# Differential attention: order of the key's sum of squares, a weight conversion and a weight split within a head

## The reference

```
q, k, v = split(h @ w_in, 3)                      # 8 heads, q and k in two halves of 64
q = rms_norm(q, q_g);  k = rms_norm(k, k_g)       # over each half's 64 features
q1, q2, k1, k2 = partial_rope(...)                # rotary on 16 of the 64
a = softmax(mask(q1 k1^T / 8)) - lam * softmax(mask(q2 k2^T / 8))
o = rms_norm(a @ v, sub_g) * (1 - lam_init)       # per head
out = o @ w_out
```

## Time and profile before

| | us |
|---|---|
| median of 3 runs | 2301.11 (2300.15 to 2301.57) |
| profiled execution, device time | 2300.4 |
| its span, first to last instruction | 2298.6 |
| PE matmul busy | 2221.3 (97%) |
| PE weight load busy | 1756.8 (76%) |
| DVE busy | 1391.9 (61%) |
| ACT busy | 795.7 (35%) |

### The profile page before, as it was taken

The page is one execution under the profiler, slowest core; times in us unless marked ns, Lnnn a source line. Parts: engine busy times, 40 slices in busy tenths (PEclk is TensorE's granted clock), DMA queues, the critical chain, the costliest instruction groups (busy, mean ns, idle before and its releaser), DMA issues.

```text
span 2298.6 us, 28503 instructions
## 1 busy us (share of the span) xinstructions
PE 2221.3 (97%) x10128; PEld 1756.8 (76%) x10128; DVE 1391.9 (61%) x2100; ACT 795.7 (35%) x1161; POOL 0.2 (0%) x4
## 2 busy tenths in 40 slices
PE   7999999999999999999999999989899999999998
PEld 5777688888886666788888867777678888888886
DVE  5666654554447776655454475577754557888744
ACT  4445432222225554322222223446622323222222
POOL 0000000000000000000000000000000000000000
PEclk9999999999999999999999999999999999999999
DMA  4111133333331111233333322222223332333332
GB/s 128 55 55 55 46 92 101 91 100 90 99 96 56 55 55 46 78 96 99 96 96 95 100 66 65 53 59 65 55 81 103 92 98 87 99 100 93 94 101 87
DMA packets 368642, 188.29 MB, mean 82 GB/s; under 512 B 8968, under 2 KB 368313, under 8 KB 368569
## 3 DMA queue, kind: packets, MB, share of 16 engines
q1 hardware_dynamic: 368569, 187.30, 28.5%
HBM read 185.18 MB, written 2.10 MB: 81 GB/s over the span
## 4 chain that ended last, share of the span: by engine, by line
PE 83%; DVE 10%; ACT 4%; issue 3%; DMA 0%; DVEq 0%; SPq 0%; ACTq 0%
PE lin L1548 73%; PE S L1572 1%; DVE dmax L992 1%; PE ob L1603 1%; ACT w_hi L520 1%; PE S L1585 1%; DVE conv L1256 1%; PE ob L1697 1%; DVE w_lo L877 1%; PE S L1811 1%; PE S L1590 1%; PE S L1575 1%; DVE prob L1005 0%; PE ob L1837 0%; DVE q_raw L1014 0%
## 5 line engine op out<-in xcount | busy, mean ns | idle before, releaser
L520 ACT ACTIVATE w_hi<-raw 128x1024 fp32r<-128x1024 f32 x361 | 381.0, 1056 | 825.4 <-PE lin L1548 817.3
L877 DVE TENSOR_TENSOR w_lo<-raw,w_hi 128x1024 fp32r<-128x1024 f32 x361 | 441.0, 1222 | 207.4 <-ACT w_hi L520 206.5
L1548 PE MATMUL lin<-h_hi,w_hi 128*128 128x512 f32 x1928 | 498.1, 400 | 7.4 <-DVE exact L1435 2.8
L1548 PE MATMUL lin<-h_lo,w_hi 128*128 128x512 f32 x1928 | 480.5, 391 | 0.0
L1548 PE MATMUL lin<-h_hi,w_lo 128*128 128x512 f32 x1928 | 478.3, 390 | 0.0
L1548 PEld LDWEIGHTS lin<-h_hi,w_hi 128*128 128x128 f32 x1928 | 362.3, 190 | 95.4 <-issue 14.1
L1548 PEld LDWEIGHTS lin<-h_hi,w_lo 128*128 128x128 f32 x1928 | 360.9, 188 | 74.8 <-issue 0.5
L1548 PEld LDWEIGHTS lin<-h_lo,w_hi 128*128 128x128 f32 x1928 | 360.2, 188 | 74.8 <-issue 0.8
L1548 PE MATMUL lin<-gu_lo,w_hi 128*128 128x512 f32 x528 | 131.4, 389 | 0.0
L1548 PE MATMUL lin<-gu_hi,w_lo 128*128 128x512 f32 x528 | 131.4, 389 | 0.0
L1548 PE MATMUL lin<-gu_hi,w_hi 128*128 128x512 f32 x528 | 131.4, 389 | 0.0
(11 more groups left out here) (311 smaller groups left out, 2241.8 us busy)
## 6 DMA issues: line engine op xcount, KB each, us to landing
raw<-in_w_in_dram SPq DMA_DIRECT2D x108, 512.0 KB, 3.8
raw<-in_w_gate_dram SPq DMA_DIRECT2D x44, 512.0 KB, 3.7
raw<-in_w_up_dram SPq DMA_DIRECT2D x44, 512.0 KB, 3.8
raw<-in_ffn_up_dram SPq DMA_DIRECT2D x44, 512.0 KB, 3.8
raw<-in_w_down_dram SPq DMA_DIRECT2D x32, 512.0 KB, 3.8
raw<-in_w_out_dram SPq DMA_DIRECT2D x24, 512.0 KB, 3.8
raw<-in_ffn_down_dram SPq DMA_DIRECT2D x16, 512.0 KB, 3.9
raw<-in_w_down_dram SPq DMA_DIRECT2D x16, 384.0 KB, 3.3
```

Of the source, the lines that this page charges most:

```text
L520: act.activation(w_hi[u.slot][:, :, :], raw[u.slot][:, :, :], ACT.Copy).then_inc(hi_ready, 1)
L877: dve.tensor_tensor(w_lo[u.slot][:, :, :], raw[u.slot][:, :, :], w_hi[u.slot][:, :, :].bitcast(f32), ALU.subtract).then_inc(lo_ready, 1)
L1548: ins = pe.matmul(acc, (wh, wh, wl)[part][:, k, :], (hi, lo, hi)[part][:, k0 + k, :], start=first and part == 0 and k == 0, stop=last and ...
```

## The change

Three pieces of queue order move, one on each of ACT, DVE and PE; no instruction is added or removed. On ACT `hi(u + 3)` goes behind `keep_turned(n, 3)`. On DVE `split(u + 2)` goes behind `mix(n, 2)`. On PE `qk_sum(n + 1, 1)` goes behind `turn_diff(n, 3)` and the value's product part 1, directly ahead of `weigh`. Head 7 keeps its order.

```diff
@@ ACT, head
                     keep_turned(n, 2)
                     if not last:
                         qk_square(n + 1, 1)
+                    keep_turned(n, 3)
+                    if not last:
                         hi(u + 3)
-                    keep_turned(n, 3)
-                    if not last:
                         qk_scale(n + 1, 1)
@@ DVE, head
                     maxima(n, 3)
+                    mix(n, 2)
                     if not last:
                         split(u + 2)
-                    mix(n, 2)
                     mix(n, 3)
@@ PE, head
                     turn_diff(n, 2)
                     if not last:
                         linear(n + 1, 2, (0,))
+                    turn_diff(n, 3)
+                    if not last:
+                        linear(n + 1, 2, (1,))
                         qk_sum(n + 1, 1)
-                    turn_diff(n, 3)
-                    if not last:
-                        linear(n + 1, 2, (1,))
                     weigh(n, last)
```

More of the change, by code:

```diff
@@ L645, in head @@
                         qk_square(n + 1, 1)
-                        hi(u + 3)
                     keep_turned(n, 3)
                     if not last:
+                        hi(u + 3)
                         qk_scale(n + 1, 1)
@@ L1737, in head @@
                         linear(n + 1, 2, (0,))
-                        qk_sum(n + 1, 1)
                     turn_diff(n, 3)
@@ L1741, in head @@
                         linear(n + 1, 2, (1,))
+                        qk_sum(n + 1, 1)
                     weigh(n, last)
```

## The result

| | before | after |
|---|---|---|
| median of 4 runs, us | 2301.22 (2300.15 to 2301.57) | 2284.94 (2283.82 to 2286.33) |
| profiled execution, us | 2300.4 | 2286.33 |
| its span, us | 2298.6 | 2284.5 |
| mean granted clock of PE in it | 0.988 | 0.988 |
| first scores of head 1 to first scores of head 7, us | 172.83 | 161.56 |

The ratio is 0.9935, with an interval of 0.992 to 0.9949. The heads' part of it, the last row, came out at 11.27 us, where the steps gave 9.35 + 1.80 = 11.15.

What follows compares the result with a forecast made beforehand. PE sets the pace and loses time by waiting. Heads 1 to 5 save 5 x 1.87 = 9.35 us, head 6 1.80, head 0 1.35, head 7 0: together 12.5, from 2301.1 to 2288.6 us; range 2286.0 to 2293.0.

Steps and rivals of the forecast that it cites:

- `diff` 2 from the last small maximum: DVE, head 3: `diff` 2 ends 1.59 us after the last small maximum's start, as in head 7, 1.14 us earlier.
- split of DVE costs `diff` 3: DVE: with the split behind `mix` 2, `diff` 3 still ends at 801.20; cost taken as 0, upper bound 0.2 us.
- `turn_diff` 3 waits for `diff` 3: PE, head 3: `turn_diff` 3 could start at 801.13 but `diff` 3 allows 801.33, so about 0.2 us of wait stays.
- `q_sq` ahead of `qk_sum`: PE, head 3: `q_sq` ends at 803.07, `qk_sum` is reached at 803.61; slack 0.4 us, the 1.39 us wait covered.
- a head: PE, heads 1 to 5: `weigh` starts at 804.57 instead of 806.44, so each head gets shorter by 1.87 us.
- head 0 / head 6: PE: head 0, which had no first wait, saves 1.35 us; head 6 saves 1.80 us.
- The step on ACT: ACT: block 3's copy ends at 803.6; behind `w_hi` it would end at 804.6, making `weigh` wait some 0.1 us.
- The unmeasured pair: PE: `qk_sum` to `weigh`, no such pair in the earlier trace; taken as 0.96 us, bounds 0.96 and 1.12.
- Rival (1): DVE's split edit brings nothing, `diff` 2 comes when it came: 9.7 us saved, 2291.4; chance 0.14 including what lies between.
- Rival (2): Gain given back in the next head: late key normalisation delays `kb`, and `scores` waits; 2301 us, chance 0.05.
- Rival (3): PE's granted clock falls and the kernel gets slower; two heads' worth gives 2315 us; chance 0.03.
- The labelled idle time: PE's labelled waits, 7.8 + 2.4 = 10.2 us, the most the change could free by labels (2290.9); start times say 12.5.

Runs made afterwards that it cites:

- The two larger comparisons: The changed kernel run again twice with no edit, against the kernel before: medians 2286.14 and 2285.45 against 2299.91 and 2298.89 us.
- two of the experiments: Against the kernel before: DVE's edit alone, ratio 1.0006; DVE's edit with `qk_sum` right behind `turn_diff` 2, parts 0 and 1 behind `turn_diff` 3, ratio 1.0109.
- the version with both splits late: Changed kernel with `split(u+2)` behind `mix` 3 and the key's `qkv_tile`, `split(u+1)` behind `mix` 0, 1 and the query's: medians 2283.51 and 2282.44 us.

## Why the prediction was right, and where it was off

| step | predicted | measured |
|---|---|---|
| `diff` 2 from the last small maximum | 1.59 | 1.62 |
| split of DVE costs `diff` 3 | 0 (to 0.2) | `diff` 3 4.39 us behind the small maximum, 4.36 before |
| `turn_diff` 3 waits for `diff` 3 | 0.20 | 0.14 |
| its transpositions | 0.35 | 0.41 |
| `qk_sum` to `weigh` | 0.96 (to 1.12) | 0.85 |
| `q_sq` ahead of `qk_sum` | 0.4 | 0.6 |
| copy of block 3 ahead of `weigh` | 1.0 | 1.0 |
| a head | 1.87 | 1.87 to 1.89 |
| head 0 / head 6 | 1.35 / 1.80 | 1.39 / 1.87 |
| all seven heads | 12.5 | 12.7 |

The 1.87 to 1.89 are the differences of the six heads' lengths. The mechanism was right in each of its steps: what waited, what covered it, what was late next (`diff` 3, not `q_sq`). The 1.81 us that I took for every part ahead of a transposition holds for the key's part 2 but not for the value's part 0, which takes 1.93; so PE reaches `turn_diff` 3 later and waits less, with the same end. The step on ACT named a wait of some 0.1 us in the old order, and the run without the edit showed 0.26. The unmeasured pair, `qk_sum` ahead of `weigh`, came out at 0.85 us, 0.11 below the lower of my two bounds, which was the pair ahead of transpositions; I had no bound from below.

That a head agrees to 0.02 us is partly luck. With 1.93 in place of 1.81 the wait for `q_sq` was 3.20 - 1.93 = 1.27 us and not 1.39; the sum's 0.85 instead of 0.96 gives the 0.11 back, and the run with PE's edit alone shows both together, 1.36 us a head. Likewise the four transpositions cost 0.06 more than I took, and the three ahead of part 0 took 0.06 less.

What was off is the step from the heads to the median, which put the scatter of the runs at nothing. The range bounded the order alone and left out the clock: one execution of this kernel moves by some 1.6 us for each 0.001 of mean granted clock, and 48 runs of the kernel before lay between 2292.8 and 2304.1. The 3.7 us between the forecast of 2288.6 and 2284.94 come apart so. The base, 2301.1, was the median of three runs and lies 0.8 us above that of the 48 later ones. The heads gave 0.2 more. The first four runs of the changed kernel lie 1.2 us below the 12 later ones. The last 1.5 us is what the later medians differ by beyond the heads' 12.7; at equal clock some 0.7 of it is left, and that stays open. The two larger comparisons gave 13.8 and 13.4 us, within what the range allowed. By the 3.7 us seen here, a range for a single comparison should have been wider by about 3 us on either side.

Rival (1), that the split edit brings nothing, is wrong as stated but holds for that edit alone. Its price of 9.7 us fits the run with PE's edit alone: 8.15 + 1.39 = 9.5 us in the heads, 10.0 at equal clock. Rival (2) did not come: `kb` was ready 3 us ahead of the scores. Rival (3) did not come either, with a clock of 1.00 through heads 1 to 6. Yet its mechanism is real in this stage, and two of the experiments ran into it: not where transpositions bunched, but where PE stood for 2 to 4 us in one piece.

The labelled idle time gave 10.2 us and the start times 12.5; 12.7 were measured in the heads. Matmul busy went from 26.34 to 27.90 of 28 us, which leaves 0.1 us, and the version with both splits late still took 0.5 us a head from there. The Trainium skill (Perfetto Trace Analysis, Identifying the Most-Contended Engine) warns that the matmul's busy share is not a good measure of how close TensorE is to roofline. These traces agree.

## What to carry to other kernels

When two waits of the bottleneck engine follow each other and the second ends at a time that another engine sets, removing the first by itself pays nothing, and it can be followed by a fall of the clock, as in two heads here; move the cover and the cause together, and look for what is late next before moving either. Count a wait from start to start, against the same pair of instructions elsewhere in the trace where nothing is waited for. A filler that nobody needs soon, like a split or a conversion for a unit of the next head, belongs behind whatever the bottleneck engine waits for, on every queue.

## What the runs showed of the hardware that was not expected

In the traces of this stage the granted clock fell to the 1.2 GHz level in two of the five heads with a wait of 2.0 us in one piece (0.84 over 830 to 839 us), in six of the seven heads with one of 3.0 to 3.7 us by the label, and in no head from 1 to 6 where the 2.0 us stood in two pieces or where the one piece was 1.5 us. The same head 7 took 16.6 or 18.0 to 18.2 us, with a clock of 1.00 or 0.86 in its first 12 us, whatever the order ahead of it. And the scatter between executions, 11 us for the kernel before, follows the mean granted clock: 1.64 us for each 0.001, correlation -0.94 over 124 runs.
